# A one-core MoE encoder layer on Trainium2: rows gathered already transposed, gates carried by a transposed one-hot, fewer interruptions between expert matmuls, and separate PSUM banks for the first pair

## The chip, the cores and the metric

The kernel runs on one core of one Trainium2 chip. The metric is device time in microseconds (us) of one execution, lower is better; the time of a kernel is the median of several executions. TensorE (PE) multiplies, VectorE (DVE) and ScalarE (ACT) work on what it left in PSUM, GpSimd (POOL) and SyncE (SP) issue most of the transfers.

## The reference, cut to what matters

One layer over 320 frames (256 of a prompt, 64 of a running stream) of 1024 features: a combined input projection, windowed attention and a short convolution, an output projection, then a mixture of 32 experts of which each frame takes four. The change touches the experts alone:

```
def _moe(x2d, w_router, b_router, w_gu, b_gu, w_down, b_down):
    logits = (x2d @ w_router) + b_router
    top_logits, top_idx = lax.top_k(logits, TOP_K)          # 4 of 32
    gates = jax.nn.softmax(top_logits, axis=-1)
    ...
    def expert_block(args):
        xe, e = args
        gu = xe @ w_gu[e] + b_gu[e]                         # 1024 -> 2048
        g, u = gu[:, :D_FF], gu[:, D_FF:]
        g = jnp.minimum(g, SWIGLU_LIMIT)
        u = jnp.clip(u, -SWIGLU_LIMIT, SWIGLU_LIMIT)
        h = (u + 1) * (g * jax.nn.sigmoid(SWIGLU_ALPHA * g))
        return h @ w_down[e] + b_down[e]                    # 1024 -> 1024
    ...
    yrows = yb.reshape(rows, d) * row_gate[:, None]
    return jnp.zeros_like(x2d).at[row_token].add(yrows)
```

All data are float32. The expert weights are 12 MiB per expert, 384 MiB in all.

## The kernel before

**Weights.** The experts go in 16 pairs. An expert's weights are 12 chunks of 1 MiB: eight of w_gu (one for each 128 rows of the contraction, `gate_up`) and four of w_down (`down`). SyncE loads the 384 chunks in the order `ORDER` (L285) into a ring of 17 slots: for pair j the 16 gate-up chunks, both experts in turn, then the 8 down chunks of pair j-1. From chunk 17 on, chunk n is issued when chunk n-17 has been used (`chunk_used`, L371). Before the experts the ring's memory holds the projection weights, so only 2 chunks can go before `v_done`, three more before `bch_done`, six more before `out_done`, and the last six of the first 17 after it (L363 to L369).

**One pair on TensorE** (L748 to L796). A chunk pair is one step of 8 float32 instructions for each expert: the even expert's 64 rows use one half of the array's columns and the odd expert's the other, and both run at once. Between the steps of the pair's gate-up stand visits of other work: after k=1 and k=2 `gather` for pair j+1, after k=4 `turn_xe`, after k=1 to 6 one `scatter` of pair j-2 each (in pair 0 `spread_b_down` instead). In the down steps `turn_gu` follows m=0, and `turn_pair` follows m=1.

**Gather.** DVE marks a one-hot `oh` (token by slot, 64 slots for each expert); TensorE multiplies it as weights with the normalized rows `hn`, 512 columns at a time, into rows `xe` (slot by feature); ACT copies them to SBUF; TensorE turns them in eight transposes; DVE copies the result to `xT`, which the gate-up steps take as weights.

**After the gate-up** ACT copies all 2048 columns to `gu_sb`, `turn_gu` turns them, DVE adds the bias and clips, ACT takes the sigmoid, DVE forms `he`, the weights of the down steps. `turn_pair` turns the one-hot of the pair (marked again) and multiplies it with the gates, which gives each slot's gate. ACT scales the down result by it to `y_hi`, DVE forms the remainder `y_lo`, `scatter` multiplies both with the turned one-hot, and DVE adds the result to `x`.

**First and last pair.** The order ahead of the first expert step is: projection, router, one-hot of the first pair, gather, copy, transposes, copy (L671 to L678, L1307). All gate-ups use PSUM banks 0 to 3, so after pair 0 TensorE waits for the copy and turns before pair 1's steps. In the last pair `scatter_last` of the pair before stands between m=2 and m=3.

Of the kernel before, what the change touches and what calls it, by code (L numbers as in the profile page):

```python
# [14 lines left out]
P = 128  # L15
# [13 lines left out]
def hybrid_layer_kernel(nc, x_prompt, x_sample, cache_k, cache_v, state_conv, norm1_g, w_in, q_norm_g,  # L29
# [40 lines left out]
    with ctx:  # L70
# [21 lines left out]
        def sem(name):  # L92
# [32 lines left out]
        sg = work_region.put("sg", FT, 2 * CAP)  # L125
# [3 lines left out]
        xe = work_region.put("xe", D)  # L129
        oh = work_region.put("oh", NT, 2, CAP)  # L130
        ohT = work_region.put("ohT", NT * P, dt=F32R)
        ge = work_region.put("ge", FT, 2 * CAP, at=8192)
# [23 lines left out]
        gatesT = work_region.put("gatesT", NT * P, rows=NE)  # L156
        b_dn = work_region.put("b_dn", D, rows=NE, at=24576)
# [39 lines left out]
        gate_col = sb("gate_col", [P, NT])  # L197
        gate_row = sb("gate_row", [P, 2])
# [35 lines left out]
        gates_turned, gatesT_ready, b_spread, b_added = (sem(n) for n in (  # L234
            "gates_turned", "gatesT_ready", "b_spread", "b_added"))
        oh_ready, oh_again, oh_turned, ohT_ready = (sem(n) for n in (
            "oh_ready", "oh_again", "oh_turned", "ohT_ready"))
        xe_done, xe_copied, xe_turned, xT_ready = (sem(n) for n in (
            "xe_done", "xe_copied", "xe_turned", "xT_ready"))
        gu_copied, gu_turned = sem("gu_copied"), sem("gu_turned")  # L240
# [30 lines left out]
        GU = ps[:, 0:4, :]  # L271
        TU = ps[:, 0:4, :].rearrange("p a n -> p (a n)").rearrange("p (a f c) -> p a f c", a=2, c=2 * CAP)
        Y = ps[:, 4:6, :]
        XE_FIRST = ps[:, 0:2, :]
        XE = ps[:, 4:6, :]
        XT = ps[:, 4:6, :].rearrange("p a n -> p (a n)").rearrange("p (k c) -> p k c", c=2 * CAP)
        OT = ps[:, 6, :]
        Y_LAST = ps[:, 0:2, :]
        LAST_BANK = [2, 3, 4, 5, 6, 7]
# [114 lines left out]
        def _(pool):  # L394
# [10 lines left out]
            pool.dma_start(bias_rows[:, :], b_gu[0]).then_inc(bias_in, 16)  # L405

# [20 lines left out]
            pool.wait_ge(out_done, 2 * NT)  # L427
# [4 lines left out]
        def _(pe):  # L432
# [961 lines left out]
```

## Time and profile before

| | us |
|---|---|
| median of 3 executions | 1155.26 |
| lowest, highest | 1147.75, 1155.85 |
| profiled execution | 1149.38 |
| span of the profiled execution, first to last instruction | 1147.7 |
| TensorE busy | 1082.7 (94%) |
| VectorE, ScalarE busy | 277.3, 131.7 |
| read from HBM | 418.81 MB |

The span is divided into 40 slices of 28.7 us in the profile's page. A matmul is pipelined and its end is modelled, so TensorE shown busy is not TensorE at its peak. The profiled execution has its own time, 1.7 us more than its span.

### The profile page before, as it was taken

What the parts mean: (1) busy time and instruction counts of PE and PEld (TensorE: products, weight loads), DVE (VectorE), ACT (ScalarE), POOL (GpSimd) and SP (SyncE); (2) the same over time, 40 slices, a digit from 0 to 9 for tenths busy, and PEclk for the clock granted to TensorE, in tenths of its full rate; (3) what the DMA queues carried; (4) which work ended last, traced back from release to release, by engine and by line L of the source; (5) the groups of instructions that cost most, each with busy time, mean ns of one, the idle gap of its engine ahead of it and who ended that gap; (6) DMA issues with size and microseconds to landing.
All of it is one profiled execution on the core that took longest, in us unless ns stands there. A gap on an engine that the chain in (4) does not pass through costs nothing.

```text
span 1147.7 us, 10950 instructions
## 1 busy us (share of the span) xinstructions
PE 1082.7 (94%) x4701; PEld 445.1 (39%) x4702; DVE 277.3 (24%) x416; ACT 131.7 (11%) x218; POOL 8.7 (1%) x22
## 2 busy tenths in 40 slices
PE   5999988989999999999999999989999999899886
PEld 4766543333333333343434343333333333333333
DVE  2543213121222212121212121212212121212131
ACT  2222111011101010101010101001010010101010
POOL 1000100000000000000000000000000000000000
PEclk9999997999999999999999999999999999999999
DMA  9910605899999999999999999999999999999994
GB/s 345 328 57 1 243 1 225 343 364 398 421 421 420 422 421 422 421 421 421 421 421 421 421 422 421 421 423 421 421 421 421 422 421 421 422 420 422 421 421 161
DMA packets 61329, 421.14 MB, mean 367 GB/s; under 512 B 6768, under 2 KB 7068, under 8 KB 12096
## 3 DMA queue, kind: packets, MB, share of 16 engines
q1 hardware_dynamic: 60208, 418.93, 89.0%
q0 software_dynamic: 576, 1.34, 0.5%
q8 instruction: 39, 0.64, 0.2%
q10 hardware_dynamic: 496, 0.15, 0.1%
q14 instruction: 10, 0.08, 0.0%
HBM read 418.81 MB, written 1.58 MB: 366 GB/s over the span
## 4 chain that ended last, share of the span: by engine, by line
PE 72%; DMA 25%; ACT 1%; DVE 1%; issue 1%; DVEq 0%; SPq 0%; ACTq 0%
PE ps L686 32%; DMA ring<-in_w_gu_dram 20%; PE ps L645 8%; PE ps L701 8%; DMA ring<-in_w_down_dram 5%; PE ps L577 5%; PE ps L733 4%; PE ps L608 4%; PE ps L479 2%; PE ps L652 2%; PE ps L712 1%; PE ps L549 1%; PE ps L688 1%; PE ps L745 1%; PE ps L488 0%
## 5 line engine op out<-in xcount | busy, mean ns | idle before, releaser
L686 PE MATMUL ps<-ring,xT 128*64 128x512 f32 x1024 | 465.0, 599 | 27.0 <-DMA ring<-in_w_gu_dram 24.1
L688 PE MATMUL ps<-ring,xT 128*64 128x512 f32 x1024 | 465.6, 599 | 0.0
L686 PEld LDWEIGHTS ps<-ring,xT 128*64 128x64 f32 x1024 | 131.5, 137 | 304.4 <-issue 302.6
L701 PE MATMUL ps<-ring,he 128*64 128x512 f32 x480 | 216.2, 596 | 4.8 <-DMA ring<-in_w_down_dram 4.7
L703 PE MATMUL ps<-ring,he 128*64 128x512 f32 x480 | 216.5, 596 | 0.0
L1305 DVE TENSOR_TENSOR x<-ps,x 128x512 f32<-128x512 f32 (+1 forms) x96 | 65.5, 686 | 365.6 <-PE ps L733 334.2
L688 PEld LDWEIGHTS ps<-ring,xT 128*64 128x64 f32 x1024 | 131.5, 137 | 0.0
L701 PEld LDWEIGHTS ps<-ring,he 128*64 128x64 f32 x480 | 62.5, 137 | 127.6 <-issue 125.5
L645 PE MATMUL ps<-hn,oh 128*128 128x512 f32 (+1 forms) x192 | 98.6, 635 | 1.1 <-DVE oh L1227 1.1
L989 ACT COPY gu_sb<-ps 128x2048 f32<-128x2048 f32 x16 | 29.8, 1865 | 352.5 <-PE ps L688 352.5
L703 PEld LDWEIGHTS ps<-ring,he 128*64 128x64 f32 x480 | 62.5, 137 | 0.0
L645 PEld LDWEIGHTS ps<-hn,oh 128*128 128x128 f32 (+1 forms) x192 | 31.7, 190 | 65.9 <-issue 64.7
L1296 DVE SCALAR_TENSOR_TENSOR y_lo<-ps,gate_row,y_hi 128x1024 fp32r<-128x1024 f32 x16 | 20.6, 1284 | 138.7 <-ACT y_hi L1005 138.7
L1274 DVE TENSOR_TENSOR ge<-ps,b_guT 128x1024 f32<-128x1024 f32 x16 | 19.6, 1225 | 120.1 <-PE ps L712 120.1
L986 ACT COPY xe<-ps 128x1024 f32<-128x1024 f32 x16 | 16.2, 1012 | 258.4 <-PE ps L645 258.4
L608 PE MATMUL ps<-w_o,mixT 128*128 128x512 f32 (+1 forms) x96 | 43.7, 613 | 0.0
L733 PE MATMUL ps<-y_hi,ohT 128*128 128x512 f32 x84 | 41.9, 499 | 0.0
L1266 DVE COPY xT<-ps 128x1024 f32<-128x1024 f32 x16 | 19.6, 1225 | 81.8 <-PE ps L652 81.8
L712 PEld LDWEIGHTS ps<-ident,gu_sb 128*128 128x128 f32 x256 | 31.9, 209 | 15.1 <-issue 15.1
L733 PEld LDWEIGHTS ps<-y_hi,ohT 128*128 128x128 f32 x84 | 15.7, 187 | 56.2 <-issue 56.2
L712 PE MATMUL ps<-ident,gu_sb 128*128 128x128 f32 x256 | 34.9, 289 | 2.1 <-ACT gu_sb L989 2.1
L577 PE MATMUL ps<-xnT,w_chc 128*128 128x320 f32 x128 | 36.5, 438 | 0.0
(190 smaller groups left out, 641.2 us busy)
## 6 DMA issues: line engine op xcount, KB each, us to landing
ring<-in_w_gu_dram SPq DMA_DIRECT2D x256, 1024.0 KB, 26.4
ring<-in_w_down_dram SPq DMA_DIRECT2D x128, 1024.0 KB, 26.7
w_chc<-in_w_in_dram SPq DMA_DIRECT2D x1, 4096.0 KB, 13.5
w_qkv<-in_w_in_dram SPq DMA_DIRECT2D x1, 3072.0 KB, 15.2
w_b<-in_w_in_dram SPq DMA_DIRECT2D x1, 2048.0 KB, 18.9
w_o<-in_w_out_dram SPq DMA_DIRECT2D x2, 1024.0 KB, 22.0
w_o<-in_w_out_dram SPq DMA_DIRECT2D x1, 2048.0 KB, 23.5
x<-in_x_prompt_dram SPq DMA_DIRECT2D x1, 1024.0 KB, 5.4
```

The source lines that it names most:

```text
L479: last = mm(ps[:, QK_BANK[i], 0:TOK], cols, xnT[:, k, :], start=(k == 0), stop=(k == KT - 1))
L577: last = mm(ps[:, BCH_BANK[part], 0:TOK], w[:, k, col:col + P], xnT[:, k, :], start=(k == 0), stop=(k == KT - 1))
L608: last = mm(ps[0:n, OUT_BANK[t][half], :], mixT[:, j, t0:t0 + n], w_o[:, j, half * HALF:(half + 1) * HALF], start=(j == 0), stop=(j == MIX ...
L645: last = mm(out[:, half, :], oh[0:m, t, :, :].rearrange("p s c -> p (s c)"), hn[0:m, t, half * HALF:(half + 1) * HALF], start=(t == 0), st ...
L686: even = mm(GU[0:CAP, n, :], xT[j % 2][:, k, 0:CAP], ring[:, first % RING, cols], start=(k == 0), stop=(k == KT - 1))
L688: odd = mm(GU[CAP:P, n, :], xT[j % 2][:, k, CAP:P], ring[:, second % RING, cols], start=(k == 0), stop=(k == KT - 1))
L701: even = mm(out[0:CAP, half, :], hid[:, f, 0:CAP], ring[:, first % RING, cols], start=(f == 0), stop=(f == FT - 1))
L703: odd = mm(out[CAP:P, half, :], hid[:, f, CAP:P], ring[:, second % RING, cols], start=(f == 0), stop=(f == FT - 1))
L712: last = nc.tensor.transpose(TU[:, part, f, :], gu_sb[:, features(part, f)], ident[:, :])
L733: last = mm(ps[:, 6 + half, :], ohT[:, t * P:(t + 1) * P], y[:, half * HALF:(half + 1) * HALF], start=(y is y_hi), stop=(y is y_lo))
L989: nc.scalar.copy(gu_sb[:, :], GU.rearrange("p a n -> p (a n)")).then_inc(gu_copied, 1)
L1305: V.tensor_tensor(x[0:m, t, cols], ps[0:m, bank, :], x[0:m, t, cols], ALU.add).then_inc(told, 1)
```

## The change

Six things are altered. (1) `gather` takes `hn` as weights and `oh` as the moving operand, 128 columns at a time, so that the rows arrive transposed; `xe`, its copy and `turn_xe` go. ACT and DVE copy a half of the result each. GpSimd clears the unused rows of `hn` for this. (2) DVE marks a second one-hot `ohg`, multiplied by the gates; `turn_oh` turns it, and DVE takes the gate of each slot as the sum of a row and the plain one-hot as what is above zero (`split_ohT`). The matmuls with the gates go. (3) Scatters stand in pairs after k=1, 3, 5, the gather's halves after k=3 and 5, and `turn_oh` right behind `turn_gu` after m=0. (4) Pair 0 has PSUM banks 0 to 3 for its gate-up and all others 4 to 7; pair 0's `turn_gu` moves behind pair 1's k=1, and the gates are turned inside pair 0. (5) The bias of the down projection is added with the scatter of pair 6, and its load waits for the counts. (6) ACT copies the gate half of `gu` and DVE the up half; in the last pair `scatter_last` of the pair before follows m=0.

The diff, cut to its core (names of semaphores, buffer sizes and the rounds for experts with over 64 rows left out; the scale and the split of y only lose their buffer index):

```diff
+        ohg = work_region.put("ohg", NT, 2, CAP)
...
+        def gu_banks(j):
+            return ps[:, 0:4, :] if j == 0 else ps[:, 4:8, :]
...
+        def gathered_banks(j):
+            first = (0, 4)[j] if j < 2 else 2
+            return ps[:, first:first + 2, :].rearrange("p a n -> p (a n)").rearrange("p (k c) -> p k c", c=2 * CAP)
+        Y = ps[:, 2:4, :]
+        OT = ps[:, 1, :]
+        GT = ps[0:NE, 7, 0:NT * P]
+        Y_LAST = ps[:, 4:6, :]
+        LAST_BANK = [2, 3, 0, 1, 6, 7]
+        BIASED = 6
...
+            pool.wait_ge(consts, 3)
+            pool.memset(hn[DEC:P, NT - 1, :], 0.0).then_inc(hn_padded, 1)
...
-            pool.wait_ge(out_done, 2 * NT)
+            pool.wait_ge(counts_ready, 2)
...
-            def gather(out, halves, tiles=range(NT)):
-                for half in halves:
+            def gather(j, half, tiles=range(NT), experts=2):
+                out = gathered_banks(j)
+                for k in range(half * KT // 2, (half + 1) * KT // 2):
                     for t in tiles:
-                        m = TT[t][1]
-                        last = mm(out[:, half, :], oh[0:m, t, :, :].rearrange("p s c -> p (s c)"),
-                                  hn[0:m, t, half * HALF:(half + 1) * HALF], start=(t == 0), stop=(t == NT - 1),
-                                  skip_group_check=True)
+                        last = mm(out[:, k, 0:experts * CAP], hn[:, t, k * P:(k + 1) * P],
+                                  oh[:, t, 0:experts, :].rearrange("p s c -> p (s c)"),
+                                  start=(t == 0 and k % (KT // 2) == 0), stop=(t == NT - 1), skip_group_check=True)
                 return last
-            def turn_xe():
-                for k in range(KT):
-                    last = nc.tensor.transpose(XT[:, k, :], xe[:, k * P:(k + 1) * P], ident[:, :])
-                last.then_inc(xe_turned, 1)
...
-            gather(XE_FIRST, (0, 1), (2,)).then_inc(xe_done, 1)
-            pe.wait_ge(rank_ready, 1)
-            for t in range(NT):
-                last = nc.tensor.transpose(ps[0:NE, 7, t * P:(t + 1) * P], gates[:, t, :], ident[:, :])
-            last.then_inc(gates_turned, 1)
-            pe.wait_ge(xe_copied, 1)
-            turn_xe()
+            for half in range(2):
+                gather(0, half, (2,)).then_inc(gathered, 1)
+            def turn_gates():
+                pe.wait_ge(rank_ready, 1)
+                for t in range(NT):
+                    last = nc.tensor.transpose(GT[:, t * P:(t + 1) * P], gates[:, t, :], ident[:, :])
+                last.then_inc(gates_turned, 1)
...
+            def turn_gu(told, banks):
+                for part, copied in enumerate((g_copied, u_copied)):
+                    pe.wait_ge(copied, told)
...
+            def turn_oh(told):
+                pe.wait_ge(ohg_ready, told)
                 for t in range(NT):
-                    nc.tensor.transpose(OT[:, t * P:(t + 1) * P], oh[:, t, :, :].rearrange("p s c -> p (s c)"),
-                                        ident[:, :])
-                for t in range(NT):
-                    m = TT[t][1]
-                    gate = cols(t, m)
-                    w = gate.shape[-1]
-                    last = mm(OT[:, NT * P:NT * P + w], oh[0:m, t, :, :].rearrange("p s c -> p (s c)"), gate,
-                              start=(t == 0), stop=(t == NT - 1), skip_group_check=True)
+                    last = nc.tensor.transpose(OT[:, t * P:(t + 1) * P], ohg[:, t, :, :].rearrange("p s c -> p (s c)"),
+                                               ident[:, :])
                 last.then_inc(oh_turned, 1)
...
+            def scatter(j, u):
                 t, half = u // 2, u % 2
+                cols = slice(half * HALF, (half + 1) * HALF)
                 for y in (y_hi, y_lo):
-                    last = mm(ps[:, 6 + half, :], ohT[:, t * P:(t + 1) * P], y[:, half * HALF:(half + 1) * HALF],
-                              start=(y is y_hi), stop=(y is y_lo))
+                    last = mm(ps[:, half, :], ohT[:, t * P:(t + 1) * P], y[:, cols],
+                              start=(y is y_hi), stop=(y is y_lo and j != BIASED), skip_group_check=True)
+                if j == BIASED:
+                    last = mm(ps[:, half, :], gatesT[:, t * P:(t + 1) * P], b_dn[:, cols], start=False, stop=True,
+                              skip_group_check=True)
                 last.then_inc(scattered, 1)
...
-                pe.wait_ge(xT_ready, j + 1)
-                if j == 0:
-                    pe.wait_ge(gatesT_ready, 1)
-                else:
+                pe.wait_ge(xT_front, j + 1)
+                pe.wait_ge(xT_back, j + 1)
+                if j >= 2:
                     pe.wait_ge(u_biased, j)
                 for k in range(GUC):
                     gate_up(j, k)
-                    if k in (1, 2) and j + 1 < PAIRS:
+                    if k == 1:
+                        if j == 0:
+                            turn_gates()
+                        if j == 1:
+                            turn_gu(1, gu_banks(0))
+                    if k in (1, 3, 5) and j >= 2:
                         if k == 1:
+                            pe.wait_ge(ohT_ready, j - 1)
+                            pe.wait_ge(yl_ready, j - 1)
+                            if j - 2 == BIASED:
+                                pe.wait_ge(gatesT_ready, 1)
+                                pe.wait_ge(b_down_in, 16)
+                        else:
+                            pe.wait_ge(added, 2 * NT * (j - 2) + k - 1)
+                        scatter(j - 2, k - 1)
+                        scatter(j - 2, k)
+                    if k in (3, 5) and j + 1 < PAIRS:
+                        if k == 3:
                             pe.wait_ge(oh_ready, j + 2)
-                            if j >= 2:
-                                pe.wait_ge(yl_ready, j - 1)
-                        last = gather(XE, (k - 1,))
-                        if k == 2:
-                            last.then_inc(xe_done, 1)
-                    if k == 4 and j + 1 < PAIRS:
-                        pe.wait_ge(xe_copied, j + 2)
-                        turn_xe()
-                    if j >= 2 and 1 <= k <= 2 * NT:
-                        u = k - 1
-                        if u == 0:
-                            pe.wait_ge(yl_ready, j - 1)
-                            pe.wait_ge(ohT_ready, j - 1)
-                        if u >= 2:
-                            pe.wait_ge(added, 2 * NT * (j - 2) + u - 1)
-                        scatter(u)
-                    if j == 0 and 1 <= k <= 2 * NT:
-                        spread_b_down(k - 1)
+                            if j == 1:
+                                pe.wait_ge(u_biased, 1)
+                        gather(j + 1, (k - 3) // 2).then_inc(gathered, 1)
                 if j == 0:
-                    pe.wait_ge(xT_ready, 2)
-                    turn_gu(1)
                     continue
                 pe.wait_ge(he_ready, j)
                 if j + 1 < PAIRS:
-                    pe.wait_ge(xT_ready, j + 2)
+                    pe.wait_ge(xT_front, j + 2)
+                    pe.wait_ge(xT_back, j + 2)
                 else:
                     pe.wait_ge(yl_ready, j - 1)
                 for m in range(DNC):
                     down(j - 1, m)
                     if m == 0:
-                        turn_gu(j + 1)
-                    if m == 1:
-                        pe.wait_ge(oh_again, j)
+                        turn_gu(j + 1, gu_banks(j))
                         if j == 1:
-                            pe.wait_ge(b_added, 2 * NT)
+                            pe.wait_ge(u_biased, 1)
                         else:
                             pe.wait_ge(added, 2 * NT * (j - 1))
-                        turn_pair(j - 1)
+                        turn_oh(j)
...
             for m in range(DNC):
                 down(L, m, he_last, Y_LAST)
                 if m == 0:
-                    pe.wait_ge(oh_again, PAIRS)
                     pe.wait_ge(ohT_ready, L)
-                    turn_pair(L)
-                if m == 2:
+                    turn_oh(PAIRS)
                     pe.wait_ge(yl_ready, L)
                     pe.wait_ge(ohT_ready, PAIRS)
                     scatter_last(y_hi, ohT, True, False)
...
+            def copy_xT(told, j):
+                act.wait_ge(gathered, 2 * told - 1)
+                nc.scalar.copy(xT[j % 2][:, 0:KT // 2, :], gathered_banks(j)[:, 0:KT // 2, :]).then_inc(xT_front, 1)
+            def copy_g(banks):
+                nc.scalar.copy(gu_sb[:, 0:FF], banks[:, 0:2, :].rearrange("p a n -> p (a n)")).then_inc(g_copied, 1)
+            def sigmoid(told, j):
                 act.wait_ge(g_ready, told)
...
+            def mark_gates(told, e, experts=2):
+                V.tensor_tensor(
+                    ohg[:, :, 0:experts, :],
+                    row_ids[:, :].unsqueeze(1).unsqueeze(1).to_broadcast([P, NT, experts, CAP]),
+                    rank[:, :, bass.ds(e, experts)].unsqueeze(3).to_broadcast([P, NT, experts, CAP]), ALU.is_equal
+                    ).then_inc(ohg_step, 1)
+                dve.wait_ge(ohg_step, told)
+                V.tensor_tensor(ohg[:, :, 0:experts, :], ohg[:, :, 0:experts, :],
+                                gates[:, :, bass.ds(e, experts)].unsqueeze(3).to_broadcast([P, NT, experts, CAP]),
+                                ALU.mult).then_inc(ohg_ready, 1)
+            def split_ohT(told, to):
+                dve.wait_ge(oh_turned, told)
+                V.tensor_reduce(gate_row[:, :], OT[:, 0:NT * P], AX.X, ALU.add).then_inc(gate_ready, 1)
+                V.tensor_scalar(to[:, :], OT[:, 0:NT * P], 0.0, None, ALU.is_gt).then_inc(ohT_ready, 1)
+            def copy_xT(told, j):
+                dve.wait_ge(gathered, 2 * told)
+                V.tensor_copy(xT[j % 2][:, KT // 2:KT, :], gathered_banks(j)[:, KT // 2:KT, :]).then_inc(xT_back, 1)
+            def copy_u(banks):
+                V.tensor_copy(gu_sb[:, FF:FLAT], banks[:, 2:4, :].rearrange("p a n -> p (a n)")).then_inc(u_copied, 1)
```

## Rows read from the trace of the kernel before

**Rows 1.** The page: TensorE's busy time, 40 slices of clock and traffic, the chain by engine.

```profile
PE 1082.7 (94%) x4701; PEld 445.1 (39%) x4702; DVE 277.3 (24%) x416; ACT 131.7 (11%) x218; POOL 8.7 (1%) x22
...
GB/s 345 328 57 1 243 1 225 343 364 398 421 421 420 422 421 422 421 421 421 421 421 421 421 422 421 421 423 421 421 421 421 422 421 421 422 420 422 421 421 161
...
PE 72%; DMA 25%; ACT 1%; DVE 1%; issue 1%; DVEq 0%; SPq 0%; ACTq 0%
```

**Rows 2.** Windows: length, busy of five engines, clock granted, DMA share, GB/s.

```profile
194.00:196.00 2.00, 0.62 (x4) 0.21 (x5) 1.49 (x2) 0.00 (x0) 0.00 (x0) 0.50 0.43 176
...
195.00:201.00 6.00, 5.21 (x18) 1.71 (x20) 1.20 (x2) 0.00 (x0) 0.00 (x0) 0.69 0.01 5
201.00:280.00 79.00, 75.38 (x310) 25.91 (x308) 13.43 (x16) 6.28 (x6) 0.00 (x0) 1.00 0.92 364
280.00:400.00 120.00, 120.00 (x540) 45.02 (x538) 29.68 (x35) 13.05 (x15) 0.00 (x0) 1.00 1.01 421
...
202.00:204.00 2.00, 2.00 (x12) 0.56 (x8) 0.00 (x0) 0.00 (x0) 0.00 (x0) 1.00 0.73 279
```

**Rows 3.** Windows of one pair's length, in the middle and late.

```profile
416.81:473.20 56.39, 56.39 (x250) 20.72 (x250) 13.49 (x16) 5.62 (x7) 0.00 (x0) 1.00 1.01 421
...
824.92:884.51 59.59, 56.96 (x250) 21.04 (x250) 13.48 (x16) 5.62 (x7) 0.00 (x0) 1.00 1.01 421
```

**Rows 4.** The chain in order of time: start, us, what; one of each kind.

```profile
45.64 5.46 PE ps L488 x48
...
204.34 2.97 PE ps L645 x6
207.31 1.05 PE ps L745 x2
...
283.31 2.12 PE ps L712 x16
...
306.99 0.66 PE ps L733 x2
...
322.70 1.03 PE ps L652 x8
```

**Rows 5.** Groups by shape: the weight loads of the gather.

```profile
L645 PEld LDWEIGHTS ps<-hn,oh 128*128 128x128 f32 x128 | 21.8, 189 | 40.9 <-issue 40.9
```

**Rows 6.** Timeline around the first expert step, and its second step's first and last instruction.

```profile
187.56 3.78 PE L645 MATMUL ps<-hn,oh 64*128 64x512 f32 x4 [1.05 <-DVE oh L1227]
...
192.44 1.97 PE L652 MATMUL ps<-ident,xe 128*128 128x128 f32 x8 [0.35 <-ACT xe L986]
...
194.51 1.23 DVE L1266 COPY xT<-ps 128x1024 f32<-128x1024 f32 x1 [6.50 <-PE ps L652]
...
195.79 1.11 PE L686 MATMUL ps<-ring,xT 128*64 128x512 f32 x1 [1.38 <-DVE xT L1266]
...
200.74 0.59 PE L686 MATMUL ps<-ring,xT 128*64 128x512 f32 x1
...
203.75 0.59 PE L686 MATMUL ps<-ring,xT 128*64 128x512 f32 x1
```

**Rows 7.** Timeline of the last pairs' down steps.

```profile
1105.28 0.55 PE L717 MATMUL ps<-ident,oh 128*128 128x128 f32 x3
...
1106.41 0.64 PE L701 MATMUL ps<-ring,he 128*64 128x512 f32 x1
...
1115.88 0.61 PE L701 MATMUL ps<-ring,he_last 128*64 128x512 f32 x1 [1.31 <-DMA ring<-in_w_down_dram]
...
1129.38 1.67 PE L804 MATMUL ps<-y_hi,ohT 128*128 128x512 f32 x6
...
1132.37 0.64 PE L701 MATMUL ps<-ring,he_last 128*64 128x512 f32 x1
```

**Rows 8.** Two windows in the last pair: between down steps, and the end of the traffic.

```profile
1114.00:1116.00 2.00, 0.69 (x6) 0.15 (x4) 0.16 (x1) 1.11 (x1) 0.00 (x0) 1.00 1.01 422
...
1130.00:1132.00 2.00, 2.00 (x10) 1.64 (x9) 0.00 (x0) 0.00 (x0) 0.00 (x0) 1.00 0.03 8
```

More of the change, by code:

```diff
@@ L665, in _ @@
             pe.wait_ge(first_marked, 1)
-            gather(XE_FIRST, (0, 1), (0, 1))
+            pe.wait_ge(hn_padded, 1)
+            for half in range(2):
+                gather(0, half, (0, 1))
             logits(2)
@@ L706, in down @@
                 odd.then_inc(chunk_used, 1)
-            def turn_gu(told):
-                pe.wait_ge(gu_copied, told)
-                for part in range(2):
+            def turn_gu(told, banks):
+                for part, copied in enumerate((g_copied, u_copied)):
+                    pe.wait_ge(copied, told)
                     for f in range(FT):
-                        last = nc.tensor.transpose(TU[:, part, f, :], gu_sb[:, features(part, f)], ident[:, :])
+                        last = nc.tensor.transpose(by_feature(banks)[:, part, f, :], gu_sb[:, features(part, f)],
+                                                   ident[:, :])
@@ L830, in again @@
                 pe.wait_ge(oh_ready, n + PAIRS)
-                gather(XE, (0, 1)).then_inc(xe_done, 1)
-                turn_oh(lambda t, m: gate_col[0:m, t:t + 1])
-                pe.wait_ge(xe_copied, n + PAIRS)
-                turn_xe()
-                pe.wait_ge(xT_ready, n + PAIRS)
+                for half in range(2):
+                    gather(PAIRS, half, experts=1).then_inc(gathered, 1)
+                turn_oh(n + PAIRS)
+                pe.wait_ge(xT_front, n + PAIRS)
+                pe.wait_ge(xT_back, n + PAIRS)
+                GU = gu_banks(PAIRS)
                 for k in range(GUC):
@@ L859, in again @@
                     for y in (y_hi, y_lo):
-                        last = mm(ps[:, 6 + half, :], ohT[0:CAP, t * P:(t + 1) * P],
+                        last = mm(ps[:, half, :], ohT[0:CAP, t * P:(t + 1) * P],
                                   y[0:CAP, half * HALF:(half + 1) * HALF], start=(y is y_hi), stop=(y is y_lo))
@@ L995, in copy_ohT @@
-            def copy_ohT(told, b, to):
-                act.wait_ge(oh_turned, told)
-                nc.scalar.copy(to[:, :], OT[:, 0:NT * P])
-                for s in range(2):
-                    half = slice(s * CAP, (s + 1) * CAP)
-                    last = nc.scalar.copy(gate_row[half, b:b + 1], OT[half, NT * P + s:NT * P + s + 1])
-                last.then_inc(ohT_ready, 1)
-            def scale_y(told, b, rows):
-                act.wait_ge(ohT_ready, told)
-                A(y_hi[:, :], rows.rearrange("p a n -> p (a n)"), ACT.Copy, scale=gate_row[:, b:b + 1]
+            def copy_xT(told, j):
+                act.wait_ge(gathered, 2 * told - 1)
+                nc.scalar.copy(xT[j % 2][:, 0:KT // 2, :], gathered_banks(j)[:, 0:KT // 2, :]).then_inc(xT_front, 1)
@@ L1273, in biased @@
                     bias = b_guT[:, part * FT:(part + 1) * FT, bass.ds(e, experts)].unsqueeze(3)
-                    return V.tensor_tensor(to_e, TU[:, part, :, :].rearrange("p f (s c) -> p f s c", c=each),
+                    return V.tensor_tensor(to_e,
+                                           by_feature(banks)[:, part, :, :].rearrange("p f (s c) -> p f s c", c=each),
                                            bias.to_broadcast([P, FT, experts, each]), ALU.add)
```

205 lines of the change are left out of this document (95 added, 110 removed).

## The prediction

> **What bounds the kernel now.** The page's busy shares come first [rows 1]: TensorE is busy 94% of the span and holds 72% of the chain, which looks like a TensorE-bound kernel. The traffic in the same 40 slices says otherwise. From the eleventh slice (287 us) to the last but one it stands at 421 GB/s, flat, whatever TensorE does. The windows confirm it: DMA share 1.01 from 280 us on [rows 2]. Two windows of one pair's length show the switch [rows 3]. In the middle a pair takes 56.39 us with TensorE never idle; late it takes 59.59 us with TensorE idle for 2.6. A pair's 24 chunks of 1 MiB are 25.17 MB, at 421 GB/s 59.8 us. So TensorE is quicker than the weights, but it started late and works off full slots until past the middle of the span, and then it waits for chunks. The transfers are the bound all the way from 280 us. Time can be won only where they stand still: before 280 us, and after the last chunk has landed.
>
> How much they stand still there [rows 2]: the first 17 slots are full at about 194.8 us (194 to 196: 176 GB/s, so 0.84 us of traffic). Then nothing moves until TensorE has used its first chunk pair (195 to 201: 5 GB/s). 202 to 204 carries 279, or 1.3 us of full rate, so the stream is back at about 202.5 us. From 201 to 280 us the mean is 364: 57 x 79 = 4503 KB short of 421. Of these (1.5 x 421 - 66 carried before 202) = 565 belong to the restart, which leaves 3938, or 9.35 us. These are later halts because a full ring waited for TensorE: in pair 0 its steps (27.4), gather (5.9), transposes (1.0), down bias (6 x 1.05), switches and slow start (2.5) [rows 4, 6] make 43 us for 16 chunks, and the stream would bring them in 39.8. At the end, traffic is gone by 1130 [rows 8], and TensorE starts the last down step at 1132.37 [rows 7].
>
> **The change, part by part.** A step of a chunk pair takes 8 x 0.43 = 3.43 us (200.74 to 203.75 are seven starts apart [rows 6]).
>
> *TensorE per pair, before:* 12 steps 41.1, gather 2 x 2.97 = 5.94, the eight transposes of `xe` 1.03, six scatters at 0.66 = 3.96, `turn_gu` 2.12 [rows 4], `turn_pair` 1.13 (1105.28 to 1106.41 [rows 7]); sum 55.3. The 1.1 to 56.39 [rows 3] are eight interruptions at 0.14 each.
>
> *After:* gather is 24 float32 matmuls with 128 moving columns, 48 instructions. The trace has this shape at L488: 48 in 5.46 us, 0.114 each [rows 4]. Lower end 48 x 0.107 = 5.1 (a step's 0.43 us for 512 columns, divided by four); upper end 48 x 0.189 = 9.1, if each load of 128x128 weights stands bare [rows 5]. I take 5.5, the same shape. The eight transposes go; `turn_oh` keeps three of them, 0.4; four interruptions are left, 0.56. Sum 41.1 + 5.5 + 3.96 + 2.12 + 0.4 + 0.56 = 53.6, 2.8 less. Even the upper end gives 57.2, still under the stream's 59.8. So for pairs 2 to 15 this is worth nothing: the transfers hide it, and TensorE reaches the state of waiting some pairs earlier.
>
> *Start of pair 0.* Before: the gather's last part at 187.56 runs 3.78 us at half clock, then copy, transposes (1.97, against 1.03 at full clock), copy (1.23), and the first step at 195.79 [rows 4, 6]. After: 16 instructions at half clock, 16 x 0.228 = 3.65, then DVE's half copy, 0.65 (half of 1.23 and a little), with ACT's half done under the second half of the gather; with 0.2 of signals the first step starts at 192.05. That is 3.7 us earlier. The turning of the gates no longer stands ahead of it. The first step took 4.95 us, partly at half clock, 1.2 GHz (195.79 to 200.74; the granted clock is 0.50 in 194 to 196 and 0.69 in 195 to 201 [rows 2, 6]); I take the same, so slots come free at 197.0 and the stream is back at 198.8 (used at 200.9, back at 202.5, so 1.6 us later). The bounds are 3.43 us (all at full clock) and 6.85 (all at half), so the stream is back between 197.1 and 200.5. The row shows half clock during the eight transposes and the rise after the step began. The Trainium skill (TensorE: Matmul & The Clock Gate, Part 4: PE-mode transpose) says that transposes don't count as activity for the clock; the new order has real products in their place, so by that rule the rise comes earlier and the start gains up to 1.5 us more, the lower bound.
>
> *Pair 0 and 1.* The 1.05 us for each two instructions of the down bias, six times [rows 4], leave pair 0 (they return as part of pair 6's scatter, 6.3 us on TensorE at most, hidden by 6 us a pair that it then has in hand). So do the copy and the turns between pairs 0 and 1. TensorE is through its steps of pair 0 at 27.4 + 5.5 + 0.5 + four or five switches + the slow 1.5 = 35.5 us after the start, 227.5. The stream needs 5 us a chunk pair. Slots come free at 197, 200.6, 204.6, 208, 214.3, 217.7, 224, 227.5, and in pair 1 at 231, 234.5, 240, 243.5, 250, 253.5, 260, 263.5; with 1.6 us of start each is ahead of the stream's 198.8, 203.8, 208.8 ... 273.5. The tightest is the second, by 1.6 us, then it grows. With a gather of 9.1 us the fifth has 2.1 us and the late ones of pair 1 still above 1. So all 9.35 us of halts go.
>
> *New waits.* DVE gets a second one-hot, a reduction and the up copy, ACT loses a copy; DVE's whole pair is 13.5 us of 56.4 [rows 3]. TensorE waits for `y_lo` after k=1: DVE has 6.9 us of steps for what is half of its pair at most, 6.7. Queued behind this wait are the scatters and the gathers. `copy_g` and `copy_u` hide under m=0 (3.43), `turn_oh` needs a one-hot marked before. Cost nothing; if one of them fails, the pair has 6 us in hand before it shows. GpSimd's memset stands ahead of stores issued long before the experts, and the down-bias load is 128 KB, 0.3 us of the stream.
>
> *Tail.* Measured from m=0 (1115.88), m=3 begins at 16.5 [rows 7]. After: m=0 3.43, `turn_oh` 0.5, `split_ohT` on DVE about 1.1 (384 columns twice, at 1.23 for 1024 [rows 6]) and 0.2 of signals, then `scatter_last` 3.1, m=1 and m=2, each 3.43: m=3 begins at 15.3, and its chunks are there by 14.3 (1130). Gain 1.2; bounds 0 and 2.1.
>
> *Sum.* 3.7 + 9.35 + 1.2 = 14.2 us. The profiled execution of 1149.38 would be 1135.2, its span 1133.5. The median of the runs shown is 5.9 above the profiled one, so the forecast is 1155.26 - 14.2 = 1141.
>
> **The rivals.**
>
> *A. TensorE's saving pays in every pair.* For it: 94% busy. Then 2.8 us in 15 pairs, 42, come on top of the start and the bias, about 12: 1101. Against it: 421 GB/s in both windows [rows 3]. If the page's 421 is no ceiling, this is right. 2%.
>
> *B. The halts stay in part.* TensorE waits once in pair 1 for `u_biased`, ahead of the third pair's gather, in banks that it shares with pair 0's turns: DVE's chain there is two adds and two clips of 1024 columns, at most 4 x 1.23 = 4.9 us, against two steps, 6.9. If the first two pairs are held up some 10 us by this or by the gather, only the earlier start and the tail remain, 5 to 9 us: 1146 to 1150. 23%.
>
> *C. The clock falls (slower).* TensorE will idle 6 us a pair instead of 2.6, in waits of up to 1.55 us between steps, from early on. At half clock a pair is 107 us against the stream's 59.8. It decides when over 12 us of a pair run at half clock (6.2 in hand). If the five steps of a pair with no visit behind them ran so, that is 17 us more, 11 over what is in hand, in some 13 pairs: 1141 + 143 = 1284. Against it: the last pair's down steps have just this rhythm, 3.43 us of work in 5, and the clock is 1.00 there [rows 8]. The Trainium skill (the same page, HAM oscillation — how this bites in real kernels) describes a kernel whose bursts between waits for transfers are throttled anew each time; by this rule C, by the row not. 4%.
>
> *D. The change doesn't do what it says:* the first step starts no earlier, because DVE or ACT is late with its half, while the halts go: 1145. It counts with B. 4%.
>
> **How the numbers follow.** The forecast has 67%, A 2%, B 23%, C 4%, D 4%. The executions shown spread over 8 us, 0.7%, so 1% (11.6 us) is about what a measurement can tell from no change. The forecast's own bounds are 11.3 (slow first step, no tail) and 16.8 us won; 1138 to 1144 from the median, and down to 1131 if the changed kernel's executions fall like the lowest one before (1147.75 - 16.8). Upward B takes it to 1149. 1131 to 1149 leaves out A, C and the end of B. Faster by over 1%: most of the forecast, and A, 65%; within 1%: B, D and the edge of the forecast, 30%; slower 5%.
>
> **What would show it.** In the profile after: 421 GB/s from the eighth slice, the halt near 195 us down to 4 us; the first step at 192; pair 0's steps over by 228; the gather's instructions at 0.114 us (not 0.19); pairs at 59.6 to 60 us from the third or fourth on, with TensorE at about 90% there; clock 1.00; last step 15.3 us after m=0. A drop of traffic under 400 between 200 and 280 would show B, a granted clock under 1.00 in any pair C. The prediction is wrong if 421 GB/s itself changes, since each 0.1% of it is 0.9 us.

## The result and the profile after

The changed kernel takes 1136.12 us (median of 4 executions, 1133.94 to 1137.46), the kernel before 1152.8 (4 executions, 1147.75 to 1155.85). The ratio of the means is 0.9858, with a 95% interval of 0.9814 to 0.9902: faster by 1.4%. The medians lie 16.7 us apart. The two profiled executions are 12.8 us apart (1149.38 and 1136.58; spans 1147.7 and 1134.9).

The page of the changed kernel, its first lines and the chain, against [rows 1]:

```profile
span 1134.9 us, 11697 instructions
...
PE 1035.9 (91%) x5053; PEld 490.7 (43%) x5054; DVE 307.3 (27%) x474; ACT 102.1 (9%) x170; POOL 9.7 (1%) x23
...
GB/s 337 335 66 1 246 1 242 424 421 420 421 422 421 421 422 421 421 421 420 422 420 421 421 421 420 421 422 421 421 421 422 420 422 421 421 421 421 420 422 141
...
PE 60%; DMA 38%; DVE 1%; SPq 1%; ACT 1%; issue 0%; DVEq 0%
```

TensorE is busy 46.8 us less, and the span is 12.8 us shorter. The traffic stands at 421 GB/s from the eighth slice on and no longer from the eleventh: slices 8 to 10 were 343, 364 and 398. In the chain TensorE's share fell from 72 to 60% and the transfers' rose from 25 to 38%.

Windows of the changed kernel, against [rows 2] and [rows 3]:

```profile
192.00:194.00 2.00, 1.73 (x8) 0.75 (x10) 0.63 (x2) 0.00 (x0) 0.00 (x0) 1.00 1.04 313
194.00:196.00 2.00, 2.00 (x12) 0.86 (x10) 0.00 (x0) 0.00 (x0) 0.00 (x0) 1.00 0.63 199
196.00:198.00 2.00, 2.00 (x12) 0.82 (x10) 0.00 (x0) 0.00 (x0) 0.00 (x0) 1.00 0.46 94
...
201.00:280.00 79.00, 79.00 (x423) 35.57 (x421) 17.79 (x21) 7.71 (x8) 0.00 (x0) 1.00 1.01 422
...
294.85:347.84 52.99, 52.99 (x274) 23.40 (x273) 15.59 (x21) 3.77 (x4) 0.00 (x0) 1.00 1.01 420
...
941.13:1000.80 59.67, 54.15 (x272) 24.19 (x272) 15.59 (x20) 3.77 (x4) 0.00 (x0) 1.00 1.01 422
```

From 201 to 280 us nothing halts any more (422 against 364). A pair that TensorE bounds takes 52.99 us (56.39 before), one that the stream bounds 59.67 (59.59 before): 3.4 us of work saved, none of it in the time.

The timeline of TensorE at the start and in the last pair, against [rows 6] and [rows 7]:

```profile
187.59 3.78 PE L652 MATMUL ps<-oh,hn 128*128 128x128 f32 x16 [1.06 <-DVE oh L1204]
192.27 0.61 PE L691 MATMUL ps<-ring,xT 128*64 128x512 f32 x1 [0.90 <-issue]
...
195.73 0.59 PE L691 MATMUL ps<-ring,xT 128*64 128x512 f32 x1
...
1102.95 0.61 PE L706 MATMUL ps<-ring,he_last 128*64 128x512 f32 x1 [1.32 <-DMA ring<-in_w_down_dram]
...
1106.54 0.55 PE L724 MATMUL ps<-ident,ohg 128*128 128x128 f32 x3
...
1108.36 1.63 PE L792 MATMUL ps<-y_hi,ohT 128*128 128x512 f32 x6 [1.27 <-DVE ohT_last L1255]
...
1118.21 0.59 PE L706 MATMUL ps<-ring,he_last 128*64 128x512 f32 x1
```

**Three intervals.** Four marks can be read from any of these traces: G, the start of the last part of the first pair's gather; K, the start of pair 0's second step, when the first ring slots have come free; M, the start of the last pair's m=0; and the end. They cut the work at the places that the prediction priced. Before: G 187.56, K 200.74, M 1115.88. After: G 187.59, K 195.73, M 1102.95.

| kernel | G | K - G | M - K | end - M |
|---|---|---|---|---|
| before | 187.56 | 13.18 | 915.14 | 31.82 |
| after | 187.59 | 8.14 | 907.22 | 31.95 |
| pair0_dose | 189.29 | 8.13 | 910.47 | 31.91 |
| gather_twice | 185.56 | 8.13 | 907.13 | 31.78 |
| gather_thrice | 190.92 | 8.14 | 967.56 | 32.08 |
| products_before_first | 190.55 | 9.13 | 907.21 | 31.41 |
| turns_before_first | 190.55 | 9.08 | 907.24 | 31.93 |
| turns_back_to_pair0 | 190.41 | 8.14 | 907.15 | 31.40 |
| tail_back | 190.59 | 8.13 | 907.28 | 33.30 |
| gather_64_rows | 187.52 | 9.66 | 907.23 | 31.89 |
| steady_clock | 187.74 | 6.40 | 907.15 | 32.01 |
| before_without_bias_visits | 185.98 | 14.73 | 911.63 | 31.76 |
| half_loads_before | 191.73 | 13.58 | 878.99 | 29.90 |
| half_loads_after | 190.64 | 8.14 | 826.60 | 31.92 |

So the 12.8 us are 5.04 + 7.92 - 0.13. M - K is 907.13 to 907.28 us in all eight kernels whose stream runs with whole chunks and does not halt after K. G, by contrast, lies anywhere between 185.6 and 190.9 us in the ten kernels with the change in which nothing ahead of it was edited (all but steady_clock), and at 187.6 and 191.7 in two with the order before. What moves it was not looked into. This is why the intervals tell more here than spans. Each profile is one execution.

### The profile page after: what moved, and what is told of

It reads as the page before. It is cut to its first block, busy times and chain, and to the rows that moved or that the text cites. A ratio compares the mean times of both kernels' runs of the same rounds, so it can differ in the third digit from the quotient of the medians.

```text
span 1134.9 us, 11697 instructions
## 1 busy us (share of the span) xinstructions
PE 1035.9 (91%) x5053; PEld 490.7 (43%) x5054; DVE 307.3 (27%) x474; ACT 102.1 (9%) x170; POOL 9.7 (1%) x23
## 4 chain that ended last, share of the span: by engine, by line
PE 60%; DMA 38%; DVE 1%; SPq 1%; ACT 1%; issue 0%; DVEq 0%
DMA ring<-in_w_gu_dram 29%; PE ps L691 24%; PE ps L706 9%; DMA ring<-in_w_down_dram 7%; PE ps L652 7%; PE ps L584 5%; PE ps L615 4%; PE ps L732 2%; PE ps L717 2%; PE ps L486 2%; DMA w_qkv<-in_w_in_dram 1%; PE ps L556 1%; PE ps L693 1%; PE ps L495 0%; SPq L351 0%; PE ps L635 0%
## 5 line engine op out<-in xcount | busy, mean ns | idle before, releaser
L691 PE MATMUL ps<-ring,xT 128*64 128x512 f32 x1024 | 456.5, 595 | 47.8 <-DMA ring<-in_w_gu_dram 46.8
L693 PE MATMUL ps<-ring,xT 128*64 128x512 f32 x1024 | 457.9, 596 | 0.0
L1303 DVE TENSOR_TENSOR x<-ps,x 128x512 f32<-128x512 f32 (+1 forms) x90 | 58.0, 684 | 338.8 <-PE ps L732 307.3
L652 PEld LDWEIGHTS ps<-oh,hn 128*128 128x128 f32 x768 | 91.7, 195 | 8.9 <-issue 5.6
L652 PE MATMUL ps<-oh,hn 128*128 128x128 f32 x768 | 93.4, 279 | 1.1 <-DVE oh L1204 1.1
L1286 DVE TENSOR_TENSOR xT<-ge,xT 128x1024 f32<-128x1024 f32 x16 | 19.6, 1225 | 110.5 <-PE ps L708 110.5
L1262 DVE COPY gu_sb<-ps 128x1024 f32<-128x1024 f32 x16 | 19.6, 1225 | 88.0 <-PE ps L693 88.0
L976 ACT COPY gu_sb<-ps 128x1024 f32<-128x1024 f32 x16 | 16.2, 1012 | 299.8 <-PE ps L693 299.8
L732 PE MATMUL ps<-y_hi,ohT 128*128 128x512 f32 x84 | 37.8, 451 | 0.0
L973 ACT COPY xT<-ps 128x512 f32<-128x512 f32 x16 | 9.4, 586 | 301.8 <-PE ps L652 301.8
L732 PE MATMUL ps<-y_lo,ohT 128*128 128x512 f32 x84 | 33.2, 395 | 0.0
```

What stands on the lines that cost most here:

```text
L652: last = mm(out[:, k, 0:experts * CAP], hn[:, t, k * P:(k + 1) * P], oh[:, t, 0:experts, :].rearrange("p s c -> p (s c)"), start=(t == 0 a ...
L691: even = mm(gu_banks(j)[0:CAP, n, :], xT[j % 2][:, k, 0:CAP], ring[:, first % RING, cols], start=(k == 0), stop=(k == KT - 1))
L693: odd = mm(gu_banks(j)[CAP:P, n, :], xT[j % 2][:, k, CAP:P], ring[:, second % RING, cols], start=(k == 0), stop=(k == KT - 1))
L732: last = mm(ps[:, half, :], ohT[:, t * P:(t + 1) * P], y[:, cols], start=(y is y_hi), stop=(y is y_lo and j != BIASED), skip_group_check=True)
L1262: V.tensor_copy(gu_sb[:, FF:FLAT], banks[:, 2:4, :].rearrange("p a n -> p (a n)")).then_inc(u_copied, 1)
L1303: V.tensor_tensor(x[0:m, t, cols], ps[0:m, bank, :], x[0:m, t, cols], ALU.add).then_inc(added, 1)
```

## The experiments

**Theory 1:** the time is the stream's: what counts is when the first slots come free, whether the stream halts after that, and what follows the last chunk. **Rival 1:** TensorE's time pays wherever it is saved. **Rival 2:** only the first step's start (and the tail) counts; pair 0 never held the stream up.

**1. More work in pair 0 (pair0_dose).**

```diff
                     gate_up(j, k)
+                    if j == 0 and 1 <= k <= 6:
+                        mm(ps[:, 6, :], ident[:, :], hn[:, 0, 0:HALF], start=True, stop=True, skip_group_check=True)
```

> The changed kernel with six extra products of 512 columns on TensorE in pair 0 alone, one after each of k=1 to 6: 6 x 1.0 us and up to four more interruptions at 0.14, 6.5 us of TensorE time. Theory 1 (only halts of the weight stream before 280 us cost time): the slots of pair 0 come free too late from the fifth chunk pair on, the stream halts 3 to 4 us in all, and the first down step of the last pair begins 3 to 4 us later than 1102.95. Rival 1 (TensorE time counts in full wherever it is): 6.5 us later. Rival 2 (only the first step's start and the tail count, pair 0 never held the stream up): 0.

Windows 201 to 280 us, and the two marks:

```profile
201.00:280.00 79.00, 79.00 (x406) 35.30 (x406) 16.37 (x20) 7.06 (x8) 0.00 (x0) 1.00 0.99 402
...
197.42 0.59 PE L691 MATMUL ps<-ring,xT 128*64 128x512 f32 x1
...
1107.89 0.61 PE L706 MATMUL ps<-ring,he_last 128*64 128x512 f32 x1 [1.30 <-DMA ring<-in_w_down_dram]
```

M - K is 910.47, 3.25 us more: half of the dose, as theory 1 worked out, and neither the 6.5 of rival 1 nor the 0 of rival 2. The ratio to the kernel before is 0.9904 (0.9869 to 0.9939), median 1142.85; the last pair begins 4.94 us later than in the changed kernel, of which 1.70 is the later G.

**2. and 3. More work in every later pair (gather_twice, gather_thrice).** The first edit repeats the gather once, the second twice:

```diff
+                        for _ in range(1 if j >= 2 else 0):
+                            gather(j + 1, (k - 3) // 2)
                         gather(j + 1, (k - 3) // 2).then_inc(gathered, 1)
```

> The changed kernel with every gather of pairs 3 to 15 executed twice (the same values written again): 5.4 us more TensorE time in each of 13 pairs, 70 us in all; a pair would need 53.0 + 5.4 = 58.4 us of TensorE against the stream's 59.7. Theory 1: span unchanged within 1.5 us, TensorE waits for chunks less and meets the stream later than 391 us. Rival 1 (TensorE's time pays in every pair): 50 to 70 us longer.

> The same gathers executed three times: 10.8 us more in each of 13 pairs, a pair 63.8 us of TensorE against 59.7. Theory 1: now TensorE is the bound from pair 2 on, the span grows by 45 to 60 us, not by twice what the doubled gather costs. Rival 1: by twice the doubled gather's cost.

One pair of gather_twice in the windows, the doubled half in its chain, and two stretches of gather_thrice:

```profile
467.86:526.21 58.35, 58.35 (x322) 28.75 (x321) 15.59 (x21) 3.77 (x4) 0.00 (x0) 1.00 1.01 421
...
467.86 5.36 PE ps L652 x48
```

```profile
500.00:600.00 100.00, 100.00 (x580) 53.19 (x578) 24.93 (x33) 5.84 (x6) 0.00 (x0) 1.00 0.95 391
600.00:700.00 100.00, 100.00 (x555) 51.28 (x551) 22.00 (x27) 5.47 (x6) 0.00 (x0) 1.00 0.96 395
```

Seventy us more TensorE work cost nothing: M - K 907.13, ratio to the kernel before 0.9844 (0.9826 to 0.9861), median 1135.29, no slower than the changed kernel. The third copy (expected at 63.8 us a pair) lifts a pair over the stream's 59.7, the traffic falls to 391, and M - K grows by 60.3, at the edge of the 45 to 60 expected; this kernel ran once. Rival 1 falls, and the point from which TensorE's time counts lies between 58.35 and 63.7 us a pair, as the stream's 59.7 says.

**4. and 5. The stream made quick (half_loads_before, half_loads_after).** From chunk 17 on half of each chunk is left out, once in the kernel before and once in the changed one (one execution each).

```diff
-                sp.dma_start(ring[:, slot, :], src).then_inc(arrived, 16)
+                w = FLAT // 2 if half else FLAT
+                sp.dma_start(ring[:, slot, 0:w], src[:, 0:w]).then_inc(arrived, 16)
```

> The kernel before with the transfers of chunks 17 to 383 cut to half their columns (the steps then multiply what an earlier chunk left there; the output is not the reference's). The stream needs half its time, so TensorE bounds every pair. Theory 1: pairs at 56.4 us throughout, span about 1115.

> The changed kernel with the same cut. Theory 1: pairs at 53.0 us throughout, span about 1050, so that the change is worth about 65 us here, against 12.8 between the two profiled executions with whole chunks: what TensorE saves per pair is there, but hidden by the stream. Rival 1b (the change saves TensorE next to nothing after pair 1): the difference stays at 13 to 17.

The chain: the same half of the gather in two successive pairs, of the first and of the second kernel:

```profile
364.99 2.97 PE ps L646 x6
...
421.38 2.97 PE ps L646 x6
```

```profile
350.89 2.68 PE ps L653 x24
...
403.88 2.68 PE ps L653 x24
```

The spans are 1114.2 and 1057.3 us, pairs 56.39 and 52.99. The change is worth 56.9 us here and 12.8 with whole chunks: what TensorE gained is real and hidden. It is 8 less than expected, because 53.0 does not hold throughout: the down bias that now rides on pair 6's scatter makes two pairs 57.58 and 55.71 us long (562.84 to 620.42 to 676.13 in this chain), 7.3 us that I had left out.

**6. One part of the gain in the kernel before (before_without_bias_visits).**

```diff
-                    if j == 0 and 1 <= k <= 2 * NT:
-                        spread_b_down(k - 1)
```

> The kernel before without the six products of the down bias in pair 0, their additions and their load (the output lacks the down bias). 6.3 us and about four interruptions less of TensorE in pair 0, which then takes 36 us against the stream's 39.8. Theory 1: of the 9.35 us of halts between 202 and 280 us 5 to 7 go, and the last pair begins 5 to 7 us earlier. Rival 2: 0, the first step's start is what counts.

M - K is 911.63, 3.5 us less than before; 5 to 7 were expected. The direction speaks against rival 2, the size is short. The estimate had left out the stop for copy and turns between pairs 0 and 1, which this kernel still has; that this is the whole of the rest is not shown. From G to M only 2.0 us are gained (926.36 against 928.32), because the first step ran almost wholly at half clock here (6.49 us, K - G 14.73). Over ten executions the ratio is 0.9955 (0.9932 to 0.9979).

**7. Pair 0's turns back (turns_back_to_pair0).**

```diff
-                        if j == 1:
-                            turn_gu(1, gu_banks(0))
...
                 if j == 0:
+                    turn_gu(1, gu_banks(0))
                     continue
```

> The changed kernel with pair 0's turns back behind its last step (own banks without use): TensorE waits for the copies, 1.2 us, and turns, 2.1, before pair 1, 3.4 to 3.6 us in all. Theory 1: the slots at the start of pair 1 come free 3.5 us later, but there the stream has over 5 us in hand: no halt, last pair unchanged within 0.5 us. Rival 1: 3.5 us later.

TensorE does stop between pairs 0 and 1:

```profile
230.56 2.18 PE L717 MATMUL ps<-ident,gu_sb 128*128 128x128 f32 x16 [1.14 <-ACT gu_sb L975]
```

Yet M - K is 907.15: no difference. Moving these turns into pair 1, which is what the separate banks are for, gains nothing once pair 0 is short.

**8. The tail (tail_back).** The scatter of the pair before stands behind m=2 again.

```diff
                     turn_oh(PAIRS)
+                if m == 2:
                     pe.wait_ge(yl_ready, L)
```

> The changed kernel with the last but one pair's scatter back between m=2 and m=3 of the last pair. Theory: the last down step begins 16.5 us after m=0 instead of 15.3, as in the kernel before, and the span is 1.2 us longer. Rival: the chunks of the last steps arrive late anyway, no difference.

m=3 begins 16.42 us after m=0 (1106.00 to 1122.42) against 15.26, and the end follows M by 33.30 us against 31.4 to 32.1 in the other kernels with the change and whole chunks.

**9. and 10. What stands ahead of the first step (products_before_first, turns_before_first).** Into a free bank:

```diff
+            for k in range(8):
+                mm(ps[:, 6, (k % 4) * P:(k % 4 + 1) * P], hn[:, 0, k * P:(k + 1) * P], ident[:, :],
+                   start=True, stop=True, skip_group_check=True)
```

```diff
+            for k in range(16):
+                nc.tensor.transpose(ps[:, 6, (k % 4) * P:(k % 4 + 1) * P], hn[:, 0, (k % 8) * P:(k % 8 + 1) * P],
+                                    ident[:, :])
```

> The changed kernel with eight extra float32 products of 128 columns (16 instructions) between the first pair's gather and its first step, in a free bank: at half clock 3.65 us, of which 0.9 lies beside the two copies. Theory 1: first step 2.8 us later (195.0), granted clock 1.00 from the first step on, the stream halts 2.8 us longer and everything up to the last pair is 2.8 us later. Rival 2b (the first 17 chunks give enough stock that the start of the first step does not matter): last pair's down step unchanged at 1102.95.

> The changed kernel with 16 extra transposes in place of the eight extra products, about as long at half clock (16 x 0.246 = 3.9 us). If transposes hold the granted clock down, as the kernel before suggests (half clock until after its first step had begun, behind eight transposes), the first step begins 3.0 us later than 192.27 and runs partly at half clock, so that its end is 4.5 to 6.5 us later than 195.7. If the kind of work does not matter for the clock, the first step runs at full clock and ends 1.5 to 3 us later.

TensorE's timeline of turns_before_first and two of its windows, then two windows of the changed kernel:

```profile
190.55 3.78 PE L652 MATMUL ps<-oh,hn 128*128 128x128 f32 x16 [1.06 <-DVE oh L1208]
194.13 2.09 PE L680 MATMUL ps<-ident,hn 128*128 128x128 f32 x16
196.14 0.64 PE L695 MATMUL ps<-ring,xT 128*64 128x512 f32 x1
...
192.00:194.00 2.00, 2.00 (x11) 2.00 (x11) 0.00 (x0) 0.59 (x1) 0.00 (x0) 0.50 0.99 418
194.00:196.00 2.00, 2.00 (x18) 1.97 (x17) 1.16 (x2) 0.00 (x0) 0.00 (x0) 0.88 1.08 403
```

```profile
191.00:192.00 1.00, 0.37 (x2) 0.08 (x1) 0.52 (x1) 0.00 (x0) 0.00 (x0) 0.50 1.01 426
192.00:193.00 1.00, 0.73 (x4) 0.40 (x6) 0.63 (x2) 0.00 (x0) 0.00 (x0) 1.00 1.14 369
```

Both miss their sizes, alike: the 16 instructions took 2.1 us, not 3.7 to 3.9, because the clock rose under them, and the first step ran at full clock, ending 0.99 and 0.94 us later than without. M - K stays, so each of these us is on the path. The step after transposes is as fast as after products. But this does not say that transposes raise the clock: 0.88 in the window 194 to 196 puts the rise at 194.5, 0.4 us after the first of them began and 3.9 us after G, and with nothing in their place it came 4.4 us after G (192.0). What does differ from the kernel before is the gather ahead of them, which the next run tries.

**11. Then what did, in the kernel before? (gather_64_rows)**

```diff
-                        last = mm(out[:, k, 0:experts * CAP], hn[:, t, k * P:(k + 1) * P],
-                                  oh[:, t, 0:experts, :].rearrange("p s c -> p (s c)"),
+                        m = TT[t][1]
+                        last = mm(out[:, k, 0:experts * CAP], hn[0:m, t, k * P:(k + 1) * P],
+                                  oh[0:m, t, 0:experts, :].rearrange("p s c -> p (s c)"),
```

> The changed kernel with the third token tile's products of every gather on its 64 real rows, as the kernel before has them, instead of 128 padded ones. Sixteen transposes behind the gather did not keep the clock down, so what did in the kernel before is open. If it was the half-empty array in the last gather part, the first step now begins or runs at half clock and takes 4.5 to 6.9 us instead of 3.45; the interval from its end to the last pair stays at 907.2. If it was the two waits of TensorE between gather and first step (0.4 and 1.4 us) or the position in time, the first step stays at 3.45 us. Pair lengths with whole chunks unchanged in both.

Its timeline and window, to be held against 192.27, 195.73 and the clock 1.00 of the changed kernel:

```profile
187.52 3.77 PE L653 MATMUL ps<-oh,hn 64*128 64x128 f32 x16 [1.06 <-DVE oh L1205]
192.19 1.08 PE L692 MATMUL ps<-ring,xT 128*64 128x512 f32 x1 [0.90 <-issue]
...
197.18 0.59 PE L692 MATMUL ps<-ring,xT 128*64 128x512 f32 x1
...
192.00:194.00 2.00, 1.81 (x6) 0.67 (x8) 0.55 (x2) 0.00 (x0) 0.00 (x0) 0.50 1.07 320
```

The gather takes the same 3.8 us and ends at the same time, but the granted clock is 0.50 (1.2 GHz) in the window where it was 1.00 (2.4 GHz), and the first step takes 4.99 us instead of 3.46. In both kernels the clock had fallen to half 2.4 us ahead of this gather. The other traces agree: 64 rows in the last gather part are followed by first steps of 4.95, 6.49 and 5.34 us (before, before_without_bias_visits, half_loads_before); 128 rows, in ten kernels, by 3.45 to 3.49. So the padding of the third token tile is worth 1.5 us, by the clock, and the half-empty array is enough for the slow first step, with no transposes and only the wait of 0.90 us that the changed kernel has too. Whether the transposes and waits of the kernel before hold the clock down further is open: the rise came 7.8 us after G here and 11.3 us after it in the kernel before, in both while the first step ran. A second place speaks for the rows in use. In gather_thrice and pair0_dose the half gather right behind pair 6's bias products, which use 32 rows, takes 4.54 and 4.57 us (703.63, 663.68) instead of the 2.94 of the changed kernel's first ones, with the granted clock at half (0.57 in 703 to 707, 0.50 in 664 to 667.4), though TensorE is never idle there.

**12. A quicker start (steady_clock).** Idle products where TensorE waits for the routing:

```diff
+            def fill(n, w):
+                for _ in range(n):
+                    mm(ps[:, 6, 0:w * P], ident[:, :], hn[:, 0, 0:w * P], start=True, stop=True,
+                       skip_group_check=True)
...
             logits(2)
+            fill(3, 2)
             pe.wait_ge(sel_ready, NT)
             ranks(RK_LAST, 2, 2, 1)
+            fill(2, 2)
```

> The changed kernel with five idle products of 256 columns in TensorE's waits while the last rows are routed (three behind the last logits, two behind the ranks), to keep the clock up. If the clock stays at full, the first pair's last gather part takes 1.9 instead of 3.8 us, the first step begins 1.9 to 2.3 us earlier (190.2), and the stream's remaining halt of 3.1 us shrinks to about 1: 2 us shorter. Rival: the products come too late or are too short for the clock, or delay the ranks: 0 to 1 us longer.

```profile
187.74 2.05 PE L652 MATMUL ps<-oh,hn 128*128 128x128 f32 x16 [0.55 <-DVE oh L1211]
...
190.69 0.61 PE L698 MATMUL ps<-ring,xT 128*64 128x512 f32 x1 [0.90 <-issue]
```

The last gather part takes 2.05 us instead of 3.78, K - G is 6.40, 1.74 less, and M - K the same. The idle products stand ahead of G, but from the last logits to G it is 4.90 us in both kernels (182.84 to 187.74, 182.69 to 187.59), so they delay nothing: by the intervals it is 1.7 us shorter than the changed kernel. The times don't show this 0.15%: the median is 1133.83 (1132.20 to 1137.18), but the ratio to the executions of the kernel before beside it is 0.9861 (0.9824 to 0.9897), no better than the changed kernel's 0.9858.

## Why the prediction was right, point by point

**The bound and the forecast.** 1141 was forecast with a range of 1131 to 1149; 1136.12 was measured. That nothing counts but halts and ends of the stream was right, and experiments 1 to 5 show it against both rivals. From the profiled executions 14.2 us were forecast and 12.8 came. That the total is so near is partly luck: the start gave 1.3 us more than its term, the halts 1.4 less, the tail 1.3 less. The forecast stood on a median of 1155.26 from three executions; with the fourth it is 1152.8, and 14.2 less is 1138.6. The medians moved by 16.7; the unprofiled executions have no traces that would say where the rest lies.

**Start of pair 0.** The first step was put at 192.05 and came at 192.27. I had charged the old first step's partly slow clock (4.95 us) and took 3.43 as the bound; it was 3.46. The lower bound had been tied to what the Trainium skill (TensorE: Matmul & The Clock Gate, Part 4: PE-mode transpose) says, that transposes don't count as activity for the clock. No run here settles that: in experiment 10 the clock would have risen without them too. The cause shown is another, the half-empty array in the gather (experiment 11). The term was 3.7 and measured 5.04.

**The halts.** 9.35 us were read from the traffic's shortfall, 7.92 came. All halts went, as stated; the term was mis-sized. Most of the 1.4 us between the two shows at the other end: from M on the kernel before still moves 5.9 MB (186 GB/s over its 31.82 us), the changed one 5.5 (173 over 31.95), 0.9 us at 421 GB/s. So the last pair begins with slightly more still to come. The shortfall is a mean over 16 transfer engines, and a chunk is there when the slowest has its part; that this is the reason is an argument, not shown. The tight place was foreseen: pair0_dose's 3 to 4 us came from the same table of slots, and it was 3.25.

**The pair.** 53.6 us was the estimate for TensorE, 52.99 it is. The gather's shape was taken from the right row: two halves of 2.68 are 0.112 us an instruction, not 0.189. The scatters, two in a row, take 1.12 us instead of 2 x 0.66, which I had not counted. Both are worth nothing here.

**New waits** cost nothing: in the window 280 to 400 us TensorE has no idle time, and with the gather doubled none up to 600 us. After that it waits for chunks alone.

**The tail.** m=3 was put 15.3 us after m=0 and comes at 15.26, 1.23 us sooner than before. But the end gives 1.36 back: from m=3 it is 16.69 us, before 15.33. What is late is the landing of the last store. The last additions end 10.5 us after m=3 begins in both kernels, the landing takes 1.3 us longer (the changed kernel's lines first, then those of the kernel before):

```profile
1125.02 3.67 DVE L1303 TENSOR_TENSOR x<-ps,x 128x512 f32<-128x512 f32 x6 [0.59 <-PE ps L792]
...
out_dram<-x SPq DMA_DIRECT2D x1, 256.0 KB, 4.3
```

```profile
1139.20 3.67 DVE L1305 TENSOR_TENSOR x<-ps,x 128x512 f32<-128x512 f32 x6 [0.59 <-PE ps L804]
...
out_dram<-x SPq DMA_DIRECT2D x1, 256.0 KB, 3.0
```

This is the step that failed: the tail's net term was +1.2 and measured -0.13. The eleven kernels with the change have 16.15 to 16.88 us from m=3 to the end, the three built on the one before 15.26 to 15.33. The moved scatter is not the cause: tail_back has the old order and 16.88 us, with a landing of 4.5. What is stays open.

**Rival C.** TensorE waits up to 1.6 us between steps, 66 us in all, and the granted clock is 1.00 in every window from 201 us on. The case that the Trainium skill describes (TensorE: Matmul & The Clock Gate, HAM oscillation — how this bites in real kernels) did not arise. The prediction had counted that section for rival C, but the kernel in it waits some 3 to 5 us for each transfer, about twice as long or more, so it is no rule for waits of up to 1.6. A trace of its kind in small is in four of the other runs: behind a single wait of 2.3 to 2.9 us for a chunk the clock fell to half for some 3 us (steady_clock at 622, turns_before_first at 628, pair0_dose at 930, tail_back at 1082 us), and M - K is no longer for it in the three without a dose (907.15 to 907.28). The rivals A and D are refuted, B too: no halt is left.

## What to carry to other kernels

Where transfers run flat at one rate for most of the span, look for the time when that begins, not at the busiest engine: 47 us of TensorE's work went and 13 us of time, all of it from the stretch of some 90 us behind the router, and none from pairs 2 to 15. Measure such a kernel between marks of its own trace, here first slots free and last pair begun (907.13 to 907.28 us), for the stage ahead of them wanders by over 5 us. The first step behind a run of short waits is worth a look at the clock: idle products there, or a full array in the work just before, moved it by 1.5 to 1.7 us.

## What the runs showed of the hardware

A gather of the same length and time with 64 rows of the array in use instead of 128 left the granted clock at 0.50 when the next work began; with 128 rows it was 1.00 (3.8 us in both, one execution each, and 3 against 8 others of that length that agree). Neither sixteen transposes nor sixteen product instructions behind such a full gather changed that (2.09 and 2.13 us). Two scatters in a row (four products) take 1.12 us where two apart take 1.32. And the first 186 to 191 us varied by 5.4 us over ten kernels with the same code there, one execution each, while 907 us of streaming varied by 0.15 over eight.
